# Where a streamed feed-forward splits its weights: new places for the second norm's slabs, for half of "up", for "down" and for the last gated rows, and a forget gate in two passes

## The reference, cut to what matters

```python
h = rms_norm(x, norm_mix); proj = h @ w_in           # parts: retention, attention, forget gate fl (8 columns), conv
logf = log_sigmoid(fl + fox_f_bias)
x = x + concat(o_ret, o_fox, o_conv) @ w_out
h2 = rms_norm(x, norm_ffn)
gate_c, new_ffn = causal_dwconv(h2 @ w_gate, hist, ffn_conv_w)
x = x + (silu(gate_c) * (h2 @ w_up)) @ w_down
```

## Time and profile before

| | us |
|---|---|
| median of 3 runs | 1673.87 (1672.96 to 1674.76) |
| profiled execution | 1675.11, of which its span 1673.1 |
| PE busy | 1616.4 (97%), 10278 matmuls |
| DVE busy | 1109.9 (66%) |
| ACT busy | 681.6 (41%) |
| POOL busy | 391.4 (23%) |
| mean granted TensorE clock | 0.995 |
| DMA queue q1, share of 16 engines | 29.9% |

### The profile page before, as it was taken

One profiled execution on the slowest core, in us unless ns is written; L12 is line 12 of the kernel. 1 busy time (PEld: TensorE's weight loads), 2 busy tenths in 40 slices (PEclk: granted clock), 3 DMA queues, 4 the chain that ended last, 5 costly groups with the idle time before them and its releaser, 6 DMA issues.

```text
span 1673.1 us, 29200 instructions
## 1 busy us (share of the span) xinstructions
PE 1616.4 (97%) x10278; PEld 1395.4 (83%) x10278; DVE 1109.9 (66%) x1760; ACT 681.6 (41%) x1273; POOL 391.4 (23%) x520
## 2 busy tenths in 40 slices
PE   7999998899999999999999999999999999999998
PEld 5758896678899999999887688866888999999997
DVE  4336446537987778888644463565298888888884
ACT  4213336414544444444332133463164444444442
POOL 1103200103433333333112040000044333333330
PEclk9999999999999999999999999999999999999999
DMA  8204421831222222222242233237222222222221
GB/s 248 75 12 109 139 89 68 279 108 51 88 85 79 75 75 79 84 90 81 73 117 63 66 79 127 85 113 270 76 64 76 75 88 87 89 87 75 75 75 68
DMA packets 125028, 160.80 MB, mean 96 GB/s; under 512 B 25604, under 2 KB 77262, under 8 KB 124622
## 3 DMA queue, kind: packets, MB, share of 16 engines
q1 hardware_dynamic: 124808, 159.44, 29.9%
q10 hardware_dynamic: 144, 0.33, 0.1%
HBM read 150.22 MB, written 9.53 MB: 95 GB/s over the span
## 4 chain that ended last, share of the span: by engine, by line
PE 75%; DVE 13%; issue 5%; DVEq 3%; ACT 2%; ACTq 1%; DMA 1%; SPq 0%; POOL 0%; POOLq 0%
PE bank L2037 70%; PE bank L2099 5%; DVE x L1865 3%; DVE wlo L1422 3%; DVE gact L1895 2%; ACTq L1362 1%; DVEq L1977 1%; DMA raw<-in_w_in 1%; DVE h L1884 1%; DVEq L1761 0%; DVE wlo L1408 0%; ACT pf L1243 0%; DVE hlo L1432 0%; DVE h L1912 0%; DVE pf L1764 0%
## 5 line engine op out<-in xcount | busy, mean ns | idle before, releaser
L2037 PE MATMUL bank<-whi,hhi 128*128 128x512 f32 x560 | 226.1, 404 | 2.7 <-DVE hlo L1432 1.6
L2037 PE MATMUL bank<-whi,hlo 128*128 128x512 f32 x560 | 220.2, 393 | 0.0
L2037 PE MATMUL bank<-wlo,hhi 128*128 128x512 f32 x560 | 219.9, 393 | 0.0
L2037 PE MATMUL bank<-hhi,whi 128*128 128x320 f32 (+1 forms) x672 | 210.4, 313 | 1.0 <-DVE hlo L1432 1.0
L2037 PE MATMUL bank<-hlo,whi 128*128 128x320 f32 (+1 forms) x672 | 209.0, 311 | 0.0
L2037 PE MATMUL bank<-hhi,wlo 128*128 128x320 f32 (+1 forms) x672 | 208.8, 311 | 0.0
L1408 DVE TENSOR_TENSOR wlo<-raw,whi 128x1024 fp32r<-128x1024 f32 (+1 forms) x84 | 98.8, 1181 | 124.1 <-ACT whi L1050 122.9
L2037 PE MATMUL bank<-whi,guhi 128*128 128x512 f32 x440 | 176.0, 400 | 3.2 <-DVE gulo L1432 2.0
L2037 PE MATMUL bank<-whi,gulo 128*128 128x512 f32 x440 | 173.6, 395 | 0.0
L2037 PE MATMUL bank<-wlo,guhi 128*128 128x512 f32 x440 | 173.5, 394 | 0.0
L1865 DVE TENSOR_TENSOR x<-x,bank 128x512 f32<-128x512 f32 x220 | 139.0, 680 | 21.6 <-PE bank L2037 21.3
(11 more groups left out here) (285 smaller groups left out, 3640.7 us busy)
## 6 DMA issues: line engine op xcount, KB each, us to landing
raw<-in_w_in SPq DMA_DIRECT2D x52, 512.0 KB, 3.6
raw<-in_w_gate SPq DMA_DIRECT2D x44, 512.0 KB, 3.7
raw<-in_w_down SPq DMA_DIRECT2D x44, 512.0 KB, 3.6
vb<-in_cache_fox_v SPq DMA_DIRECT2D x16, 1024.0 KB, 7.5
raw<-in_w_up SPq DMA_DIRECT2D x24, 512.0 KB, 3.5
gains<-in_w_up SPq DMA_DIRECT2D x20, 512.0 KB, 3.5
raw<-in_w_out SPq DMA_DIRECT2D x16, 512.0 KB, 4.8
kb<-in_cache_fox_k SPq DMA_DIRECT2D x8, 1024.0 KB, 7.0
```

Source lines behind the costliest of these rows:

```text
L2037: return pe.matmul(out, lhsT=lhsT, rhs=rhs, start=start, stop=stop, skip_group_check=True)
```

## The change

1. `wfl` holds the forget gate's hi and lo side by side (16 columns); `hhi` and then `hlo` pass over them: 2 halves x 8 blocks x 2 matmuls = 32 of 320 columns. This adds the product lo x lo. Five matmuls with the constant `fsum` (8 columns) turn and add the two groups of 8 rows, in place of the 5 transposes.
2. The norm's table is `{0: G0, 3: G0 + 1, 4: G0 + 2}` on ACT and DVE.
3. Up's first half has a home of its own, `raw_up0`, where `t2f` was; `t2f` stands behind `t3h`/`t3l` now, so a drain of DVE goes ahead of `t_low(3)`. SP's events are 4 (down's second half), 6 (gate's second half), 7, 8, 13 (up's first half), 15.
4. Down's first half is split at the beginning of the turn that uses it, behind the copy of a1 (before: at the end of the turn before), its second half behind the copy of a2 (before: ahead of it).
5. In the last turn DVE multiplies, splits the last two down slabs and then multiplies the last product; `guhi` and `gulo` are made tile by tile, the first `guhi` before the last product. The `last` transposes go to six banks (before: four in turn), and the end's banks are named by a table.

The homes, SP's loads and the norm's table:

```diff
-        (fqg, fkg, gng, t2f, qbd) = region(
+        (fqg, fkg, gng, raw_up0, qbd) = region(
...
-        (upad, ccs, t3h, t3l, kbo, flr, vm, gnd, gnsq, _, roT, lc, lcd, lexp, nct) = region(
+        (upad, ccs, t3h, t3l, _, t2f, kbo, flr, vm, gnd, gnsq, _, roT, lc, lcd, lexp, nct) = region(
...
-            src = gains[:, :] if kind == "u" and j == 1 else raw[:, s, :]
+            src = raw[:, s, :] if kind == "g" else gains[:, :] if j == 1 else raw_up0[:, :]
...
-                    for j, e in ((3, 4), (4, 6)):
-                        load(LOOP0 + j, l, ffn_src(j, it), (e, it))
-                    for j, e in ((2, 7), (0, 8), (1, 13)) if further else ():
+                    load(LOOP0 + 3, l, ffn_src(3, it), (4, it))
+                    for j, e in ((1, 6), (2, 7), (0, 8)) if further else ():
                         load(LOOP0 + j, l, ffn_src(j, it + 1), (e, it))
                     if further:
+                        wait_lo(sp, 13, l, it)
+                        apart(sp)
+                        load_up(0, it + 1)
                         wait_lo(sp, 15, l, it)
                         apart(sp)
-                        load_up1(it + 1)
+                        load_up(1, it + 1)
...
-                for j in range(3):
-                    load(LOOP0 + j, l, ffn_src(j, 0))
+                load(LOOP0, l, ffn_src(0, 0))
+                load(LOOP0 + 1, l, ffn_src(1, 0))
+                load_up(0, 0)
                 sp.wait_ge(xn_ready, l * (2 * TT) + 2 * TT)
                 apart(sp)
-                load_up1(0)
+                load_up(1, 0)
+                load(LOOP0 + 2, l, ffn_src(2, 0))
...
-                norm(1, l, {0: G0, 2: G0 + 1, 3: G0 + 2})
+                norm(1, l, {0: G0, 3: G0 + 1, 4: G0 + 2})
```

ACT, in a turn and at the end of a layer:

```diff
                     copied("g", "a1", it)
+                    down_hi(0, l, it)
                     act.wait_ge(gu_done, it + (l * PAIRS + 1))
                     act.activation(guhi[:, :, :], gu[:, :, :], ACT.Copy).then_inc(gu_hi, 1)
                     copied("g", "c1", it)
-                    B.wait_full(act, ("g", "loop", "c1"), l, it)
+                    copied("g", "a2", it)
                     down_hi(1, l, it)
-                    copied("g", "a2", it)
...
+                act.wait_ge(gu_first, l + 1)
+                act.activation(guhi[:, 0, :], gu[:, 0, :], ACT.Copy).then_inc(gu_hi_end, 1)
                 act.wait_ge(gu_done, l * PAIRS + PAIRS)
-                act.activation(guhi[:, :, :], gu[:, :, :], ACT.Copy).then_inc(gu_hi, 1)
+                act.activation(guhi[:, 1, :], gu[:, 1, :], ACT.Copy).then_inc(gu_hi_end, 1)
```

DVE, ahead of the loop, in a turn, in the last turn and at the end:

```diff
+                dve.drain()
                 t_low(3)
...
-                down_lo(0, l, 0)
...
+                    down_lo(0, l, it)
                     lo(gulo[:, :, :], gu[:, :, :], guhi[:, :, :]).then_inc(gu_ready, 1)
                     down_lo(1, l, it)
...
+                    if not further:
+                        dve.drain().then_inc(gu_first, 1)
+                        split(DLAST, l)
+                        split(DLAST + 1, l)
                     gate_lo(6)
...
-                        down_lo(0, l, it + 1)
-                    else:
-                        split(DLAST, l)
-                        split(DLAST + 1, l)
...
+                for ft in range(2):
+                    dve.wait_ge(gu_hi_end, l * 2 + ft + 1)
+                    ins = lo(gulo[:, ft, :], gu[:, ft, :], guhi[:, ft, :])
+                ins.then_inc(gu_ready, 1)
```

PE, the forget gate, and the banks of the transposes of `last`:

```diff
-                    for half in range(2):
-                        key = ("fl", half)
-                        for k in range(4):
-                            ins = mm3(bank[B.bank(key)][0:FH, 0:HALF], whi[:, s_, ws], wlo[:, s_, ws], hhi[:, 4 * i + k, ts],
-                                      hlo[:, 4 * i + k, ts], i == 0 and k == 0, i == 1 and k == 3)
+                for half in range(2):
+                    for k in range(KT):
+                        for h_ in (hhi, hlo):
+                            ins = mm(bank[B.bank(key)][0:2 * FH, 0:HALF], wfl[:, k, :, :].rearrange("p s n -> p (s n)"),
+                                     h_[:, k, ts], k == 0 and h_ is hhi, k == KT - 1 and h_ is hlo)
...
+                    ins = mm(bank[B.bank("flT")][:, t * FH:(t + 1) * FH], flr[:, t * P:(t + 1) * P], K("fsum")[0:2 * FH, :], True, True)
...
+LAST_BANKS = (0, 1, 2, 4, 5, 6)
+END_BANKS = (3, 7, 0, 1, 2, 4, 5, 6, 3, 7)
...
-        j(("last", g), g % 4)
+        j(("last", g), LAST_BANKS[g])
```

More of the change, by code:

```diff
@@ L78 @@
 for _name, _n in (("ident", P), ("cs", TT * 64), ("kdec", TT * RH), ("qdec", 2 * P), ("g16", 2), ("tri", 896),
-                  ("tris", P), ("bmask", 16), ("e0", P), ("bsel", NB)):
+                  ("tris", P), ("bmask", 16), ("e0", P), ("bsel", NB), ("fsum", FH)):
     CONST[_name] = (_at, _n)
@@ L111, in tables @@
     put("bsel", ((p % HD) // FH)[:, None] == b8[None, :])
+    put("fsum", (p[:, None] < 2 * FH) & (p[:, None] % FH == np.arange(FH)[None, :]))
     i = np.arange(SEQ)
@@ L273, in end_jobs @@
 def end_jobs():
-    return [(("d", "end", nc, t), 3 + (2 * t + nc) % 5) for t in range(TT) for nc in range(2)]
+    return [(("d", "end", nc, t), END_BANKS[2 * t + nc]) for t in range(TT) for nc in range(2)]
 def plan_banks(banks):
@@ L433, in build @@
             [("os", [P, 4, P], F32), ("ncc", [P, PAST], F32R)])
-        eb = own("eb", [P, 2, P], F32R)
+        (eb, wfl) = region([("eb", [P, 2, P], F32R)], [("wfl", [P, KT, 2, FH], F32R)])
         (fqT, fkT, fv, h11, h12, guhi, gulo, gact, t2h, t2l, s1, s2) = region(
@@ L515, in build @@
         raw_in = [sem(f"raw_in{i}") for i in range(SLOTS)]
-        up1_in = sem("up1_in")
+        up_in = [sem(f"up{i}_in") for i in range(2)]
         hi_split = sem("hi_split")
@@ L579, in build @@
         gu_done = sem("gu_done")
+        gu_first = sem("gu_first")
+        gu_hi_end = sem("gu_hi_end")
         tap_first = sem("tap_first")
@@ L654, in width, with forget_part, forget_raw @@
             return 4 * FH if n in (FL, FL + 1) else 1024
+        def forget_part(n, lo_):
+            k = 4 * (n - FL)
+            return wfl[:, k:k + 4, lo_, :]
+        def forget_raw(n):
+            return raw[:, slot(n), 0:width(n)].rearrange("p (k n) -> p k n", k=4)
         parted = sem("parted")
@@ L851, in _ @@
                 ffn_loads(PAIRS - 2, False)
-                for c, e in ((0, 8), (1, 13)):
+                for c, e in ((0, 8), (1, 6)):
                     load(DLAST + c, l, down_src(l, None, c), (e, PAIRS - 2))
@@ L1049, in split @@
                 wait_loaded(act, n, l)
+                if n in (FL, FL + 1):
+                    act.activation(forget_part(n, 0), forget_raw(n), ACT.Copy).then_inc(hi_split, 1)
+                    return
                 act.activation(whi[:, slot(n), 0:width(n)], raw[:, slot(n), 0:width(n)], ACT.Copy).then_inc(hi_split, 1)
@@ L1141, in _ @@
                 for half in range(2):
-                    evac(("fl", half), flr[:, half * HALF:(half + 1) * HALF], l, view=lambda b: b[0:FH, 0:HALF])
+                    evac(("fl", half), flr[:, half * HALF:(half + 1) * HALF], l, view=lambda b: b[0:2 * FH, 0:HALF])
                 upto(C0 + 6, l)
@@ L1906, in completed @@
                         whole(h21, "B21")
-                norm(1, l, {0: G0, 2: G0 + 1, 3: G0 + 2}, completed)
+                norm(1, l, {0: G0, 3: G0 + 1, 4: G0 + 2}, completed)
                 dve.drain()
@@ L2023, in _ @@
                 pair(PAIRS - 2, False)
-                dve.wait_ge(gu_hi, l * PAIRS + PAIRS)
-                lo(gulo[:, :, :], gu[:, :, :], guhi[:, :, :]).then_inc(gu_ready, 1)
+                for ft in range(2):
+                    dve.wait_ge(gu_hi_end, l * 2 + ft + 1)
+                    ins = lo(gulo[:, ft, :], gu[:, ft, :], guhi[:, ft, :])
+                ins.then_inc(gu_ready, 1)
                 if l + 1 == DEPTH:
@@ L2187, in _ @@
                     piece(l)
-                transposes("flT", [(bank[B.bank("flT")][:, t * FH:(t + 1) * FH], flr[:, t * P:(t + 1) * P])
-                                   for t in range(TT)], l)
+                B.wait_room(pe, "flT", l)
+                for t in range(TT):
+                    ins = mm(bank[B.bank("flT")][:, t * FH:(t + 1) * FH], flr[:, t * P:(t + 1) * P], K("fsum")[0:2 * FH, :], True, True)
+                fill(ins, "flT")
                 B.wait_all_taken(pe, [("rt", t) for t in range(TT)] + [("c", 1, t) for t in range(TT)], l)
```

49 lines of the change are left out of this document (22 added, 27 removed).

## The result

The changed kernel takes 1686.03 us (median of 4 runs, 1684.70 to 1688.11) against 1673.41 for the kernel before (4 runs): ratio 1.0073, 95% interval 1.0061 to 1.0085. It is 12.6 us slower. The forecast was +4.2, with 1684.0 as its upper end.

What follows compares the result with a forecast made beforehand. PE was taken to bound the kernel, busy 97% of the span, so only its work and gaps could move the time. Terms -4.7 + 5.8 + 1.0 + 0.5 + 1.6 = +4.2 on 1673.87 gave 1678.1 us, range 1667.5 to 1684.

Steps and rivals of the forecast that it cites:

- The clock, +1.6: End of a layer: PE's one gap of 2.2 us brings half clock, +0.8 us a layer, +1.6 us.
- forecast +2.9 each: From the norm to the first a4: the norm's +1.0 with the first turn's +1.9 us, in each layer.
- forecast +0.75 each: Steady turns and layer end: 0.05 us for each of 20 turns, and +0.25 us a layer on `gulo`.
- The forget gate, -4.7: Forget gate: sixteen matmuls fewer a layer, 2.34 us each layer, with the `fsum` matmuls replacing five transposes; -4.7 us.
- The norm, +1.0 a layer: Behind the second norm: POOL's gate sums start later and meet four of DVE's long sums, not three; +1.0 us a layer.
- The first turn, +1.9 a layer: First turn: POOL's earlier up sums meet DVE's `t3l`, `t4l` and last gate splits, three meetings ahead of a4; +1.9 us a layer.
- But a4 is the late one, on DVE: First turn: a2's 1.21 us wait for a1's copy goes, but PE's a4 waits for DVE, so that gain is swallowed.
- The steady turns, +0.05: Steady turns: down's later second split uses up the slack before a4; 0.05 us each over 20 turns, +1.0 us.
- The end, +0.25 on `gulo`, one gap: End of a layer: second `gulo` +0.25 us a layer, +0.5 in all; PE has one gap of 2.2 us.
- rival (d): The clock falls at both ends and in the first turns, 1.5 us more each time: up to 1681 us; chance 0.06.
- The side: Whole kernel: slower, +4.2 us; chance 0.45 of 1677.2 us or more.
- rival (a): Faster: POOL's sums find places where DVE is not late; 1669.7 us, about 1667 with meetings saved; chance 0.28.

Runs made afterwards that it cites:

- e4_loop: The kernel before with changes 3 and 4 alone (up's first half in raw_up0, down's splits at the turn's beginning): 1680.85 us, ratio 1.0040.
- e2_norm: The kernel before with change 2 alone, the second norm's table {0, 3, 4}: 1678.86 us, ratio 1.0021.
- g3_last_banks: The kernel before with change 5 (end by tile, six banks for the `last` transposes) but without its table of end banks: 1675.35 us, ratio 1.0002.
- e3_end: The kernel before with change 5 alone, the end of a layer, banks included: 1678.51 us, ratio 1.0030.
- f1_home: The kernel before with change 3 alone, up's first half at home in raw_up0: 1679.68 us, ratio 1.0036.
- g1_pool_wait: The changed kernel with POOL waiting ahead of the loop until the layer's first `gu` is done: 1684.65 us, ratio 1.0058 against the kernel before.

## Why the prediction was wrong

The step that failed is the clock's. "The price is that of the norm: about 1 us", taken at 0.8 a layer, gave half clock a term of +1.6, at the ends of the layers alone. The runs show about +9: each fall costs 1.7 us, and falls came in the first turns and the attention too. Next to it stands a term that was left out, the end's bank table.

To see where time went, compare when PE starts the same piece of work in both profiled executions (spans 1673.1 and 1686.1, 13.0 apart). The columns give how much longer each stretch is in the changed kernel:

| PE's stretch, up to | layer 0 | layer 1 | what it holds |
|---|---|---|---|
| the attention's fifth unit (261.70, now 257.41) | -4.3 | +3.7 | forget gate, -1.5 each. Layer 0: a start 1.3 sooner, and 1.5 from half clock at 120 to 126 that is absent now. Layer 1: half clock behind the end's gap and at 953, 1.7 each, and the bank wait, 1.8 |
| the third norm tile (396.62, now 393.83) | +1.5 | +1.3 | half clock, 3.4 in place of 1.7 |
| the first a4 (446.44, now 448.43) | +4.8 | +3.0 | forecast +2.9 each; in layer 0, 1.9 is half clock |
| the end's first matmul of down (829.34, now 832.00) | +0.7 | +0.7 | turns and `gulo`, forecast +0.75 each |
| the end of the program | | +1.6 | half clock behind the end's gap |

- **The forget gate, -4.7.** "The five small matmuls with `fsum` stand where five transposes stood" failed: 1.28 us for 0.47. On PE it is -1.5 a layer, -3.0 in all, and in time about -1 with its usual clock. (The DMA share of 0.18 named there is not in the earlier trace rows, which has 0.26 and 0.40; nothing rests on it.)
- **The norm, +1.0 a layer.** The mechanism held: POOL starts at 407.06, four meetings (407.15 and 414.77 the first and last). The size was too small: alone it measures +3.5 for both layers, and 1.6 a layer up to a4. PE's gap at the fourth tile shrank from 2.35 to 1.33 us, and a new one of 1.57 opened ahead of gate's first product. Half clock did go there, in both layers.
- **The first turn, +1.9 a layer.** Of three meetings, `t3l` and `t4l` had none (1.49 and 1.48 us); the last three gate splits took 4.46 in place of 1.97. With the norm, DVE's part is what was forecast: +3.0 in layer 1, and in layer 0 +4.8 less 1.9 of half clock, against +2.9. "But a4 is the late one, on DVE" held in layer 1 and failed in layer 0: late `gu` holds `guhi`, `guhi` holds the copies on ACT, PE stands 3.37 us at a3 and comes back at half clock. The one gap of 4 to 6 us forecast ahead of a2 came as two, 2.89 at a2 and 3.37 at a3, and the wait for a4 covered 1.5 of the 3.4 us of half clock there. I had looked at what ACT's order gives to a2, and not at what it queues behind a later `gu`. That both parts together come out at the forecast is in part luck: alone, the loop part costs 3.0 a layer there (e4_loop) and the norm 1.6 (e2_norm).
- **The steady turns, +0.05.** Held: +0.07 (38.94).
- **The end, +0.25 on `gulo`, one gap.** Held: 2.38 us. But the end's bank table had no term at all: a wait of 1.76 us, and 3.5 to 4.7 us in the end part alone (g3_last_banks against e3_end).
- **The clock, +1.6.** This is what put the time outside the range. Without its clock the forecast was +2.6, and the time at full clock rose by about 3. Three readings were wrong. The price: around's window at 0.50 the clock is low from 401 to 405, and what is lost there is 2 x (0.21 + 0.50 + 0.14) = 1.7 us, not 1. Windows of the kernel before, on either side of the one in the earlier trace rows:

```profile
400.00:402.00 2.00, 1.43 (x9) 1.23 (x10) 2.00 (x3) 1.59 (x4) 1.16 (x4) 0.79 0.44 157
...
404.00:406.00 2.00, 2.00 (x14) 2.00 (x13) 1.90 (x3) 0.00 (x0) 0.00 (x0) 0.86 0.68 225
```

The places: counted this way over the whole trace, the kernel before loses 8.5 us in five places, the changed kernel 18.7. The norms lose 3.4 less; the first turns lose 6.8 more, the ends 3.4, and the attention, which nothing in the change touches, 3.4 (low from 257 to 263, before only from 261 to 265). I had priced it only at the ends. And rival (d), with a chance of 0.06, named both ends and both first turns at 1.5 us each, which is 6, but added 3.
- **The side** was right, and for most of its reasons.
- In **rival (a)** the chance of 0.28 rested on POOL finding idle places of DVE; in the first turn neither f1_home nor g1_pool_wait shows any.

Open: why half clock follows one gap and not another of the same size (2.38 us in g3_last_banks and e3_end; at a2 in the changed kernel 2.89 us in layer 0 without it, 2.98 in layer 1 with it), why the attention has more of it in the changed kernel, and why the kernel before alone varies from 1671.2 to 1677.3 us with clocks from 0.997 to 0.993. The changed kernel with its gaps filled was not run, so no run takes the half clock away from it: its share rests on the clocks and windows above.

## What to carry to other kernels

On an in-order engine, ask of each late instruction what is queued behind it, and who waits for that: here one late `gu` held two copies behind `guhi` and opened a gap of 3.37 us on PE, which a later wait would have covered, had half clock not followed. A bank table is part of the schedule: check each reused bank against the engine that frees it last. Where windows show half clock, look at PE's longest gaps: with the lighter forget gate, filling one gap with matmuls nobody reads gave 4.0 us. Filling at a place without a gap cost 2.2 us a layer.
